# Convolution feed-forward tiles: one 512-column and one 256-column product, with the token factor applied on GpSimd

## The reference, cut to what matters

```
def conv_ffn(x, w_up, conv_w, conv_b, w_down):
    h = x @ w_up                       # 256 x 1024 @ 1024 x 5632
    h = causal depthwise conv of width 3 along the tokens, + conv_b
    gate, up = jnp.split(h, 2, axis=-1)
    return (jax.nn.silu(gate) * up) @ w_down
```

## Time and profile before

| | |
|---|---|
| median of 3 runs | 1645.68 us (1645.22 to 1650.97) |
| the profiled execution | 1649.71 us, its span 1647.9 us |
| TensorE busy | 1616.9 us, 98% |
| VectorE busy | 1200.6 us, 73% |
| ScalarE busy | 949.6 us, 58% |
| GpSimd busy | 76.4 us, 5% |
| granted TensorE clock | 0.997 of full speed |
| ffn0 in the trace | about 154 to 342 us |
| ffn1 in the trace | about 454 to 642 us |

### The profile page before, as it was taken

One profiled execution on the slowest core, in us unless ns is written; L12 is line 12 of the kernel. 1 busy time (PEld: TensorE's weight loads), 2 busy tenths in 40 slices (PEclk: granted clock), 3 DMA queues, 4 the chain that ended last, 5 costly groups with the idle time before them and its releaser, 6 DMA issues.

```text
span 1647.9 us, 30289 instructions
## 1 busy us (share of the span) xinstructions
PE 1616.9 (98%) x10649; PEld 1434.9 (87%) x10649; DVE 1200.6 (73%) x2073; ACT 949.6 (58%) x1611; POOL 76.4 (5%) x78
## 2 busy tenths in 40 slices
PE   8999999999999999999999999999999999999998
PEld 7888999998899998888879978888888889878887
DVE  5868877778577777866675877666876668776666
ACT  7465655565575556655576456555755557665554
POOL 5000000000000001000000000000090000000000
PEclk9999999999999999999999999999999999999999
DMA  9446666675356666766665556666666665446662
GB/s 267 142 129 193 203 185 184 177 163 128 88 178 182 188 184 207 237 188 188 191 198 159 185 179 193 190 189 187 173 195 188 190 189 164 132 122 205 189 190 84
DMA packets 393609, 292.68 MB, mean 178 GB/s; under 512 B 33419, under 2 KB 365476, under 8 KB 393152
## 3 DMA queue, kind: packets, MB, share of 16 engines
q1 hardware_dynamic: 390448, 280.83, 59.1%
q0 software_dynamic: 2944, 10.80, 1.9%
q10 hardware_dynamic: 144, 0.07, 0.0%
HBM read 290.59 MB, written 1.07 MB: 177 GB/s over the span
## 4 chain that ended last, share of the span: by engine, by line
PE 91%; DVE 5%; ACT 2%; issue 1%; DMA 0%; SPq 0%; DVEq 0%; ACTq 0%
PE ps L427 19%; PE ps L404 18%; PE ps L405 18%; PE ps L406 18%; PE ps L431 10%; DVE w_lo L395 1%; DVE SQ L641 1%; DVE H L647 1%; PE ps L726 1%; ACT w_hi L388 1%; PE ps L1065 1%; PE ps L514 0%; PE ps L462 0%; PE ps L463 0%; PE ps L466 0%
## 5 line engine op out<-in xcount | busy, mean ns | idle before, releaser
L395 DVE TENSOR_TENSOR w_lo<-raw,w_hi 128x1024 fp32r<-128x1024 f32 x532 | 648.3, 1222 | 31.4 <-ACT w_hi L388 29.4
L388 ACT ACTIVATE w_hi<-raw 128x1024 fp32r<-128x1024 f32 x532 | 544.0, 1049 | 46.5 <-PE ps L406 30.9
L404 PE MATMUL ps<-x_both,w_hi 128*128 128x256 f32 x1224 | 350.4, 286 | 3.0 <-DVE x_both L567 1.4
L405 PE MATMUL ps<-x_both,w_lo 128*128 128x256 f32 x1224 | 346.4, 283 | 0.0
L406 PE MATMUL ps<-x_both,w_hi 128*128 128x256 f32 x1224 | 346.3, 283 | 0.0
L427 PE MATMUL ps<-x_both,w_hi 128*128 128x512 f32 x1360 | 339.8, 391 | 1.1 <-DVE w_lo L395 1.1
L427 PEld LDWEIGHTS ps<-x_both,w_hi 128*128 128x128 f32 x1360 | 249.5, 188 | 49.4 <-DVE w_lo L395 1.3
L404 PEld LDWEIGHTS ps<-x_both,w_hi 128*128 128x128 f32 x1224 | 234.7, 192 | 8.4 <-issue 3.8
L405 PEld LDWEIGHTS ps<-x_both,w_lo 128*128 128x128 f32 x1224 | 234.9, 192 | 1.7
L406 PEld LDWEIGHTS ps<-x_both,w_hi 128*128 128x128 f32 x1224 | 234.7, 192 | 0.0
L404 PE MATMUL ps<-w_hi,h_hi 128*128 128x512 f32 x536 | 210.7, 393 | 0.1
(11 more groups left out here) (344 smaller groups left out, 1866.5 us busy)
## 6 DMA issues: line engine op xcount, KB each, us to landing
raw<-in_ffn_w_up SPq DMA_DIRECT2D x176, 512.0 KB, 3.8
raw<-in_ffn_w_down SPq DMA_DIRECT2D x132, 512.0 KB, 4.5
raw<-in_ffn_w_gate SPq DMA_DIRECT2D x88, 512.0 KB, 4.6
raw<-in_hgrn_w_in SPq DMA_DIRECT2D x32, 512.0 KB, 5.5
raw<-in_gmlp_w_in SPq DMA_DIRECT2D x32, 512.0 KB, 4.4
raw<-in_gmlp_w_out SPq DMA_DIRECT2D x16, 512.0 KB, 4.1
raw<-in_hgrn_w_out SPq DMA_DIRECT2D x8, 512.0 KB, 3.5
raw<-in_dsa_w_in SPq DMA_DIRECT2D x16, 256.0 KB, 4.5
```

Of the source, the lines that this page charges most:

```text
L388: nc.scalar.activation(w_hi[:, s, :], raw[:, s, :], ACT.Copy).then_inc(hi_done, 1)
L395: nc.vector.tensor_tensor(w_lo[:, s, :], raw[:, s, :], w_hi[:, s, :].bitcast(F32), ALU.subtract)\
L404: pe.matmul(o, whi, xhi, start=first, stop=False, skip_group_check=not group)
L405: pe.matmul(o, wlo, xhi, start=False, stop=False, skip_group_check=not group)
```

## The change

The convolution tiles take the pair form, all but the very last up tile of each feed-forward. ScalarE copies the second half of each pair tile to SBUF, VectorE adds the first half to it, and GpSimd, in a new function `conv_pool`, multiplies the sum by R in place; ScalarE's centre tap waits for that. VectorE makes both taps of the up tile before ahead of the first low split, and adds the two halves of the up tile ahead of the second. ScalarE makes all three high splits of an iteration before the centre tap of the up tile. In the last iteration the up tile is handled as before. GpSimd runs `conv_pool` for ffn0 after it has issued its table for the next stage, and for ffn1 after it has issued two loads of gains. Three semaphores of single fills become one, `fills`, to make room for the new ones (three places that wait for them, with 2, 2 and 3, are left out here).

```diff
--- before.py
+++ after.py
@@ -701,8 +701,8 @@
                     if i0 >= 2:
                         pe.wait_ge(*tile(read, f, i - 1))
                     xw = n_ if i0 == 0 and what == 0 else None
-                    if conv:
-                        mm = feat_tile(pe, ps[:, 2 * par + what, 0:L], c + what, x_wait=xw)
+                    if conv and what and i0 == NF - 1:
+                        mm = feat_tile(pe, ps[:, 2 * par + what, 0:L], c + what)
                     else:
                         mm = feat_pair(pe, ps[:, 2 * par + what, :], c + what, x_wait=xw)
                     mm.then_inc(used, 1)
@@ -816,21 +816,34 @@
                     return plain_it(i, n, i0)
                 par = i0 % 2
                 c = tile_chunk(c0, i0) + HI_AHEAD
+                act.wait_ge(used, c - HI_AHEAD + 1 + RING * n)
+                nc.scalar.activation(gs[:, par, :], ps[:, 2 * par, L:2 * L], ACT.Copy).then_inc(S("conv_half"), 1)
                 split_hi(act, c, n)
-                act.wait_ge(*tile("gate_read", f, i + 1))
+                act.wait_ge(*scaled(f, i, 0))
                 if i0 > 0:
                     act.wait_ge(*tile("silu", f, i))
                 nc.scalar.activation(ga[:, :], gs[:, par, :], ACT.Identity, scale=conv_col(2, f, i),
                                      bias=conv_col("b", f, i)).then_inc(S("gate_tap"), 1)
+                if i0 < NF - 1:
+                    act.wait_ge(used, c - HI_AHEAD + 2 + RING * n)
+                    if i0 > 0:
+                        act.wait_ge(S("conv_step"), 3 * i + 3 * NF * f)
+                    nc.scalar.activation(us[:, :], ps[:, 2 * par + 1, L:2 * L], ACT.Copy).then_inc(S("conv_half"), 1)
                 if i0 > 0:
                     high(i - 1, 1 - par)
                 act.wait_ge(*tile("conv_gs", f, i + 1))
                 nc.scalar.activation(sl[:, par, :], ga[:, :], ACT.Silu).then_inc(S("silu"), 1)
-                split_hi(act, c + 1, n)
-                act.wait_ge(*tile("up_read", f, i + 1))
+                if i0 < NF - 1:
+                    split_hi(act, c + 1, n)
+                    if i0 > 1:
+                        split_hi(act, c + 2, n)
+                    act.wait_ge(*scaled(f, i, 1))
+                else:
+                    act.wait_ge(*tile("up_read", f, i + 1))
                 nc.scalar.activation(ua[:, :], us[:, :], ACT.Identity, scale=conv_col(2, f, NF + i),
                                      bias=conv_col("b", f, NF + i)).then_inc(S("up_tap"), 1)
-                if i0 > 1:
+                if i0 == NF - 1:
+                    split_hi(act, c + 1, n)
                     split_hi(act, c + 2, n)
 
             if f == 2:
@@ -866,6 +879,33 @@
             nc.vector.tensor_tensor(h_lo[:, par, :], hid[:, par, :], h_hi[:, par, :].bitcast(F32), ALU.subtract)\
                 .then_inc(S("hid_lo"), 1)
 
+        def halved(f, i, what):
+
+            return S("conv_half"), (2 * NF - 1) * f + 2 * i + 1 + what
+
+        def scaled(f, i, what):
+
+            return S("conv_scaled"), (2 * NF - 1) * f + 2 * i + 1 + what
+
+        def conv_pool(pool, f):
+
+            pool.wait_ge(*once("r_done", FN[f]))
+
+            def scale(i, i0):
+                par = i0 % 2
+                pool.wait_ge(*tile("gate_read", f, i + 1))
+                nc.gpsimd.tensor_tensor(gs[:, par, :], gs[:, par, :], R[:, :], ALU.mult).then_inc(S("conv_scaled"), 1)
+                if i0 < NF - 1:
+                    pool.wait_ge(*tile("up_read", f, i + 1))
+                    nc.gpsimd.tensor_tensor(us[:, :], us[:, :], R[:, :], ALU.mult).then_inc(S("conv_scaled"), 1)
+
+            for i in range(3):
+                scale(i, i)
+            with pool.Fori(1, 10) as n:
+                scale(2 * n + 1, 3)
+                scale(2 * n + 2, 4)
+            scale(21, 21)
+
         def conv_dve(dve, f):
 
             c0 = start[FN[f]]
@@ -898,14 +938,12 @@
             def it(i, n, i0):
                 par = i0 % 2
                 c = tile_chunk(c0, i0)
-                gate_at = c + 1 + RING * n
-                dve.wait_ge(used, gate_at)
-                nc.vector.tensor_tensor(gs[:, par, :], ps[:, 2 * par, 0:L], R[:, :], ALU.mult).then_inc(S("gate_read"), 1)
+                dve.wait_ge(*halved(f, i, 0))
+                nc.vector.tensor_tensor(gs[:, par, :], ps[:, 2 * par, 0:L], gs[:, par, :], ALU.add).then_inc(S("gate_read"), 1)
                 if i0 > 0:
                     up_first(i)
+                    up_second(i)
                 split_lo(dve, c + AHEAD, n)
-                if i0 > 0:
-                    up_second(i)
                 dve.wait_ge(*tile("gate_tap", f, i + 1))
                 own(1, i, tap(gs[:, par, :], ga, 1, i))
                 if i0 > 0:
@@ -913,12 +951,14 @@
                 own(1, i)
                 tap(gs[:, par, :], ga, 2, i).then_inc(S("conv_gs"), 1)
                 if i0 < NF - 1:
+                    dve.wait_ge(*halved(f, i, 1))
+                    nc.vector.tensor_tensor(us[:, :], ps[:, 2 * par + 1, 0:L], us[:, :], ALU.add).then_inc(S("up_read"), 1)
                     split_lo(dve, c + 1 + AHEAD, n)
                 if i0 > 0:
                     low(dve, f, i, 1 - par)
-                dve.wait_ge(used, gate_at + 1)
-                nc.vector.tensor_tensor(us[:, :], ps[:, 2 * par + 1, 0:L], R[:, :], ALU.mult).then_inc(S("up_read"), 1)
                 if i0 == NF - 1:
+                    dve.wait_ge(used, c + 2 + RING * n)
+                    nc.vector.tensor_tensor(us[:, :], ps[:, 2 * par + 1, 0:L], R[:, :], ALU.mult).then_inc(S("up_read"), 1)
                     split_lo(dve, c + 1 + AHEAD, n)
                 if 1 < i0 < NF - 1:
                     split_lo(dve, c + 2 + AHEAD, n)
@@ -2470,18 +2510,18 @@
 
         @block.gpsimd
         def _(pool):
-            nc.gpsimd.memset(vst[:, VSTAGES - 1, :], 0.0).then_inc(S("vz"), 1)
+            nc.gpsimd.memset(vst[:, VSTAGES - 1, :], 0.0).then_inc(S("fills"), 1)
             nc.gpsimd.memset(eps6[:, :], 1e-6)
             nc.gpsimd.memset(eps5[:, :], 1e-5)
             nc.gpsimd.memset(mhalf[:, :], -0.5)
-            nc.gpsimd.memset(ones[:, :], 1.0).then_inc(S("ones"), 1)
-            pool.wait_ge(S("vz"), 1)
+            nc.gpsimd.memset(ones[:, :], 1.0).then_inc(S("fills"), 1)
+            pool.wait_ge(S("fills"), 1)
             for dst, src in vec_loads[1:]:
                 pool.dma_start(dst, src).then_inc(S("in_vec"), 16)
             pool.dma_start(cst[:, P:CCOLS], T["constants"][:, P:CCOLS]).then_inc(S("in_cst"), 16)
             pool.dma_start(pos_i[:, :], T["positions_2"].broadcast_to([P, L])).then_inc(S("in_pos"), 16)
             pool.dma_start(toe_b[:, 0:BUCKETS], T["rel_bias"].rearrange("k h -> h k"), allow_slow_non_contiguous=True).then_inc(S("in_rel"), 16)
-            nc.gpsimd.memset(Pd.rearrange("p a b c -> p (a b c)"), 0.0).then_inc(S("pd_zero"), 1)
+            nc.gpsimd.memset(Pd.rearrange("p a b c -> p (a b c)"), 0.0).then_inc(S("fills"), 1)
 
             pool.wait_ge(S("in_rel"), 16)
             for b in range(BUCKETS):
@@ -2495,6 +2535,7 @@
             pool.dma_start(toe, bass.AP(tensor=toe_dram.tensor, offset=0, ap=[[1, P], [ATT_W, NH_A], [1, L]]))\
                 .then_inc(S("in_toe"), 16)
             nc.gpsimd.memset(A[:, 8 * K1:8 * K1 + 260], 1.0).then_inc(S("ds_ones"), 1)
+            conv_pool(pool, 0)
 
             def gain(n, src):
                 pool.dma_start(gain_rows[n], src.broadcast_to([P, D])).then_inc(S("in_gain"), 16)
@@ -2502,6 +2543,7 @@
             pool.wait_ge(*rows_of("ffn1", 4))
             gain("mid", T["final_norm"].rearrange("(a d) -> a d", a=1))
             gain("p2", T["ffn_post_g_2"][0, 0:1])
+            conv_pool(pool, 1)
             pool.wait_ge(S("in_gain"), GAINS_IN["mid"])
             for tb in range(TB):
                 mid_product(pool, tb)
```

More of the change, by code:

```diff
@@ L1032, in hgrn_pe @@
                 if t == 1:
-                    pe.wait_ge(S("ones"), 1)
+                    pe.wait_ge(S("fills"), 2)
                     pe_spread(pe, "hg")
@@ L1160, in hgrn_act @@
             split_hi(act, 1)
-            act.wait_ge(S("ones"), 1)
+            act.wait_ge(S("fills"), 2)
             row_root(act, "hg")
@@ L1198, in hgrn_act @@
                 if n == 6:
-                    act.wait_ge(S("pd_zero"), 1)
+                    act.wait_ge(S("fills"), 3)
                     act.wait_ge(S("hg_pred"), 6)
```

## The result

The changed kernel takes 1662.76 us (median of 6 runs, 1660.32 to 1664.09), the kernel before 1646.85 us in its runs of the same series: a ratio of 1.0096 (95% interval 1.0086 to 1.0106), 0.96% or 16 us **slower**. The forecast was 1648.9 us in a range of 1639 to 1662. The mechanism that happened is rival A.

The account below looks back on a forecast made before the run. TensorE was taken to bound the steady part, other engines the ends. Per feed-forward 4.1 - 3.5 + 1.0, twice, gave +3.2 us on the 1645.68 median: 1648.9 us, range 1639 to 1662.

Parts of the forecast that it names:

- rival A: Convolution loop: GpSimd's up multiply waits out VectorE's whole run, delaying the next gate copy; pace 8.85, 1669 us; within 0.18.
- The tile form: Convolution feed-forwards: pair tiles save 0.19 us an iteration, 0.095 a tile, 8.2 us for both if nothing else moved.
- The price of a multiply: GpSimd's 256-column multiply by the token factor: 0.70 us, range 0.60 to 0.85.
- who waits for GpSimd's port: GpSimd and VectorE shut each other out for one whole instruction; VectorE is charged 2 x 0.70 us an iteration.
- The steady state: Middle iterations: VectorE needs 7.9 us, the other loop 7.6, so TensorE still sets the pace, at 8.31 us.
- two more rivals: New tile form no faster, 1656 us, and multiplies dearer than forecast; 0.18 together with rival A.
- The start: First iterations of each feed-forward: other engines set the pace, TensorE stalls, gate 3 starts 4.1 us later.
- The tail: Last down product of each feed-forward: its chain gains 1.24 us, 0.24 of it covered, so +1.0 us.
- The 37 tiles': Gate 3 to gate 21 of each feed-forward: 37 tiles at 0.095 us saved each, -3.5 us.
- GpSimd's queue: GpSimd's other work before and behind the two multiply loops: over in time or waiting anyway, no cost.
- the semaphores: Merging the single-fill semaphores costs nothing, since the order is unchanged.

Follow-up runs that it names:

- run with one gap: Changed kernel with one added wait on VectorE, for its own low split to end, between that split and h_lo: 1648.82 us, ratio 1.0011 to the kernel before.
- variant with the shorter run behind the add: Changed kernel with VectorE's second low split ahead of the up tile's add instead of behind it: 1663.96 us, ratio 1.0095 to the kernel before.
- next gate copy first: Changed kernel with ScalarE's copy of the next gate tile ahead of the up tile's centre tap: 1646.63 us, ratio 1.0000 to the kernel before.

## Why the prediction was wrong

**The tile form** was right: 8.50 to 8.31 wherever TensorE sets the pace, and the sum of -6.9 us for 36 iterations came out as -6.8.

**The price of a multiply** was nearly right: 0.74 us where VectorE is idle, against the forecast 0.70, and above the floor of a quarter of the undisturbed 2.39 us, 0.60. The Trainium skill's figure ("GPSIMD Engine Reference", 3.1), 4497 ns for 2048 columns, had given an estimate of 0.81, 0.07 above the measured time. A multiply that has had to wait for VectorE ends only about 0.6 us behind it; the 1024 columns show the same, 2.22 us behind the split's end (641.91 + 3.21 = 645.12 against 641.68 + 1.22 = 642.90) instead of 2.39. Little hung on this term.

**The step that failed** is "who waits for GpSimd's port": "I charge each multiply to VectorE in full: 2 x 0.70 an iteration", and with it the 0.70 for GpSimd in the loop that gave 7.6 us. It takes for granted that GpSimd gets in at the end of the one instruction it meets. It got in where VectorE waited for itself (the gate's multiply, 0.91 us, VectorE stretched by 0.35), and not at all where three instructions followed each other (3.12 us, VectorE not stretched at all): there the up tile's multiply ended 2.07 us behind the end of the low split that it met (234.30 against 231.02 + 1.22 = 232.24), and not 0.70. The two rows of before, of one such instruction each, could not tell the two cases apart, as the prediction says itself; I gave the one reading 0.50 and the other, together with two more rivals, 0.18. The run with one gap brings back the steady state of the forecast, 8.31. That it takes 1648.8 us where 1648.9 was forecast is partly luck: it is 2.0 us above the kernel before in its own series, and the forecast was 3.2 above a lower median, with gate 3 4.1 us late where this run has 3.2.

**The steady state** at 8.31 fell with it: 8.57. Rival A had the chain right, up to the copy queued behind the up tap, with 8.85 for the pace and 1669 for the time. Counted from the gate copy the multiply ended after 7.9 us (226.42 to 234.30) and not 8.2. Its parts were off: it had 6.3 for the pace, 4.5 for the start and 1.0 for the tail, where ffn0 shows 1.2, 5.9 and 0.4. The measured 1662.8 is 0.8 us outside the stated range.

**The start** had +4.1 for gate 3 and measured +3.5, mostly in the right places: TensorE waits 0.3 us before gate 2 (0.6 forecast), 1.3 before up 2 (2.0) and 1.4 before gate 3 (1.0); before down 0, where 0.8 was forecast, the view has no wait. What I missed is what follows: the fourth round took 8.4 us and not 7.5, for the same reason as the middle, so nothing was caught up and the delay of the gate reads stayed at 5.9. **The tail** had +1.0 and showed two waits for h_lo, 2.5 us together, since the gate reads already ran behind TensorE; counted from the last gate read it cost 0.4. **The 37 tiles'** -3.5 never came. **GpSimd's queue** and the semaphores cost nothing that the trace shows, as expected.

## What to carry to other kernels

Before work is moved to an engine that shares a port with another, look at what the other one issues from the moment the moved instruction becomes ready: here its delay was the run up to VectorE's next wait (or, in one variant, its next read of PSUM), not one instruction, and its end, not its length, was what counted. Then look at what is queued behind the instruction that waits for it; here a copy for the next tile stood there, and moving it ahead took the whole delay off the pace. And a form that pays where one engine sets the pace can be kept out of the iterations where it does not: the same change in 18 of 22 iterations, on the engine with time to spare, turned +16 us into -7.

## What the runs showed of the hardware

Alone, a multiply of 128 x 256 on GpSimd took 0.74 us; in the variant with the shorter run behind the add VectorE was idle beside this one, in the first iteration of ffn0:

```profile
168.50 0.42 DVE L956 TENSOR_TENSOR us<-ps,us 128x256 f32<-128x256 f32 x1
170.68 0.42 DVE L942 TENSOR_TENSOR gs<-ps,gs 128x256 f32<-128x256 f32 x1 [1.76 <-ACT gs L820]
...
169.00 0.74 POOL L900 TENSOR_TENSOR us<-us,R 128x256 f32<-128x256 f32 x1 [3.22 <-DVE us L956]
```

Where it had to wait, it ended some 0.6 us behind the end of VectorE's run in all forms seen (0.58 to 0.61 behind one tap, one split, h_lo and a split, and all three). A wait of VectorE for its own last instruction, with some 0.03 us between the two, was enough for GpSimd to get in. Once in, it held up VectorE's next instruction (h_lo 0.85 instead of 0.42, ending 0.27 behind the multiply).

A read of PSUM ended the run too, without any gap. In the fourth round with the next gate copy first, the gate add (one input in PSUM, one in SBUF) starts at 181.14, before the last split has ended, and still the multiply ends at 181.83, 0.61 behind that split; the add is not stretched either:

```profile
180.00 1.22 DVE L395 TENSOR_TENSOR w_lo<-raw,w_hi 128x1024 fp32r<-128x1024 f32 x1
181.14 0.42 DVE L947 TENSOR_TENSOR gs<-ps,gs 128x256 f32<-128x256 f32 x1
...
178.70 3.13 POOL L905 TENSOR_TENSOR us<-us,R 128x256 f32<-128x256 f32 x1 [3.65 <-DVE us L960]
```

So the run that counted in these rows was one of instructions with both inputs in SBUF.

The long power on GpSimd, 42.07 us, did nothing of the kind; a low split beside it in the kernel before (GpSimd, VectorE) had its usual length:

```profile
1195.34 42.07 POOL L2522 TENSOR_TENSOR R<-RT,mhalf 128x256 f32<-128x256 f32 x1 [22.80 <-DVE RT L969]
...
1197.12 1.22 DVE L395 TENSOR_TENSOR w_lo<-raw,w_hi 128x1024 fp32r<-128x1024 f32 x1
```

What sets a multiply apart from a power of the same size was not tried.
